# Two of eight router heads moved beside the next tile's attention, the other six on a new clock

## The reference, cut to what matters

```
def peer_ffn(h, wq, subkeys, u_tab, v_tab):      # 8 heads, 2 x 128 sub-keys, top 16 of each
    q = (hf @ wq).reshape(T, PEER_HEADS, 2, PEER_DKEY // 2)
    scores = jnp.einsum('thjd,hjkd->thjk', q, subkeys)
    top_s, top_i = lax.top_k(scores, PEER_TOPK)
    cand = top_s[:, :, 0, :, None] + top_s[:, :, 1, None, :]
    best_s, best_c = lax.top_k(cand.reshape(T, PEER_HEADS, PEER_TOPK * PEER_TOPK), PEER_TOPK)
    i1 = jnp.take_along_axis(top_i[:, :, 0], best_c // PEER_TOPK, axis=-1)
    i2 = jnp.take_along_axis(top_i[:, :, 1], best_c % PEER_TOPK, axis=-1)
    experts = i1 * PEER_KEYS + i2                 # 8 x 16 = 128 experts for each token
    gates = jax.nn.softmax(best_s, axis=-1)
    act = jax.nn.gelu(jnp.einsum('td,tkd->tk', xt, u_tab[et]))
    out = jnp.einsum('tk,tkd->td', gt * act, v_tab[et])
```

## Time and profile before

| what | value |
|---|---|
| median of three runs | 3264.56 us (3263.48 to 3269.51) |
| the profiled execution, its own time | 3259.96 us |
| its span | 3258.1 us |
| busy share of the span: PE, DVE, ACT, POOL | 72%, 72%, 46%, 36% |
| bytes by DMA, mean rate | 1317.83 MB, 404 GB/s |
| of them gathers of experts | 1073.81 MB, 1024 gathers |
| mean of one dot product on DVE (line 1870) | 1223 ns, 1024 of them |

### The profile page before, as it was taken

The page is one execution under the profiler, slowest core; times in us unless marked ns, Lnnn a source line. Parts: engine busy times, 40 slices in busy tenths (PEclk is TensorE's granted clock), DMA queues, the critical chain, the costliest instruction groups (busy, mean ns, idle before and its releaser), DMA issues.

```text
span 3258.1 us, 44723 instructions
## 1 busy us (share of the span) xinstructions
PE 2334.8 (72%) x15076; PEld 1157.1 (36%) x15076; DVE 2342.5 (72%) x6339; ACT 1496.1 (46%) x4877; POOL 1157.9 (36%) x1029
## 2 busy tenths in 40 slices
PE   7677777677775777767686678768778578866555
PEld 5363334243341434423243333424335143431111
DVE  6588856887668876688567975688766886588554
ACT  2215453355534455344543545344553446444443
POOL 0003343333433333333432434333443333334443
PEclk9788888888996988879888888878888798887777
DMA  9869999999999999999999999999999999999998
GB/s 371 362 249 380 412 421 419 404 411 420 420 418 410 404 419 383 419 402 418 421 419 416 404 420 421 419 405 406 420 413 419 403 417 421 418 414 397 422 421 341
DMA packets 206795, 1317.83 MB, mean 404 GB/s; under 512 B 26381, under 2 KB 42941, under 8 KB 53478
## 3 DMA queue, kind: packets, MB, share of 16 engines
q0 software_dynamic: 147456, 1073.81, 80.0%
q1 hardware_dynamic: 58390, 240.51, 18.5%
q10 hardware_dynamic: 720, 0.66, 0.1%
HBM read 1310.02 MB, written 7.16 MB: 404 GB/s over the span
## 4 chain that ended last, share of the span: by engine, by line
DMA 37%; PE 23%; DVE 22%; ACT 7%; issue 4%; POOL 3%; ACTq 0%; SPq 0%; POOLq 0%; DVEq 0%
DMA ringbuf<-in_p_uv,IDX 33%; PE PS L1010 12%; DVE ringbuf L1870 10%; POOL ringbuf L649 3%; PE PS L942 3%; DMA WB<-in_p_wi 3%; PE PS L786 2%; PE PS L972 2%; ACT v_th L1343 2%; ACT DIAG L1368 1%; ACT v_w L1361 1%; DVE I L1763 1%; PE PS L745 1%; DVE T L1761 1%; DVE ZB L1562 1%
## 5 line engine op out<-in xcount | busy, mean ns | idle before, releaser
L649 POOL DMA_INDIRECT ringbuf<-in_p_uv,IDX x1024 | 1157.6, 1130 | 2074.9 <-PE PS L1010 1684.2
L1010 PE MATMUL PS<-ringbuf,DIAG 64*64 64x512 f32 x8192 | 1292.3, 758 | 764.3 <-ACT DIAG L1368 734.3
L1870 DVE SCALAR_TENSOR_TENSOR ringbuf<-ringbuf,H 128x1024 f32<-128x1024 f32 x1024 | 1237.6, 1223 | 620.1 <-DMA ringbuf<-in_p_uv,IDX 611.3
L1010 PEld LDWEIGHTS PS<-ringbuf,DIAG 64*64 64x64 f32 x8192 | 310.7, 157 | 1468.5 <-ACT DIAG L1368 994.7
L1340 ACT ACTIVATE v_sq<-v_y 128x2 f32<-128x2 f32 x512 | 104.3, 204 | 1365.0 <-DVE ringbuf L1870 1334.9
L1343 ACT ACTIVATE v_th<-v_sq,v_y 128x1 f32<-128x1 f32 x1024 | 340.6, 380 | 17.2
L1361 ACT ACTIVATE v_w<-v_th,v_g 128x1 f32<-128x1 f32 x800 | 266.1, 379 | 38.4 <-ACT v_th L1343 1.1
L972 PEld LDWEIGHTS PS<-HT,WB 128*128 128x128 f32 x1856 | 222.3, 200 | 64.4 <-issue 56.6
L1368 ACT ACTIVATE DIAG<-fold,v_w 128x64 f32<-128x64 f32 x800 | 234.7, 340 | 13.0
L972 PE MATMUL PS<-HT,WB 128*128 128x128 f32 x1856 | 233.1, 286 | 2.0 <-DMA WB<-in_p_wq 2.0
L786 PE MATMUL PS<-WB,HT 128*128 128x256 f32 (+2 forms) x816 | 177.8, 373 | 48.6 <-DMA WB<-in_p_wi 48.6
(11 more groups left out here) (290 smaller groups left out, 2453.7 us busy)
## 6 DMA issues: line engine op xcount, KB each, us to landing
WB<-in_p_wq SPq DMA_DIRECT2D x58, 1024.0 KB
WB<-in_p_wi SPq DMA_DIRECT2D x37, 1024.0 KB
ringbuf<-in_p_ahead SPq DMA_DIRECT2D x20, 1024.0 KB, 10.9
WB<-in_p_ada SPq DMA_DIRECT2D x16, 1024.0 KB
WB<-in_p_wo SPq DMA_DIRECT2D x16, 1024.0 KB
ringbuf<-in_p_uv,IDX POOLq DMA_INDIRECT x1024
WF<-in_p_ada SPq DMA_DIRECT2D x12, 1024.0 KB, 13.8
WB<-in_p_wi SPq DMA_DIRECT2D x14, 768.0 KB
```

The costliest lines, as they stand in the source:

```text
L649: pool.indirect_dma_start(out=ring[n % RING], out_offset=None, in_=table, in_offset=bass.IndirectOffsetOnAxis(ap=IDX[:, k % 2, s:s + 1], a ...
L1010: mm = pe.matmul(PS[half:half + HALF, 2 * c + r, :], DIAG[r * HALF:(r + 1) * HALF, (n + q) % DIAGS, :], row[r * HALF:(r + 1) * HALF, D + c ...
L1870: dve.scalar_tensor_tensor(row, row, GELU_T, H2[:, k % 2, :], ALU.mult, ALU.mult, accum_out=Y[:, b, q:q + 1]).then_inc(dotted, 1)
```

## The change

1. The last lot (heads 6 and 7) of every tile but the last leaves `route` and becomes a generator `late` that DVE's attention loop of the next tile advances at nine of its steps (`LATE_AT`), each time behind that step's logits reduction. Its exponential on ACT moves to attention step i = 9 (`LATE_GATE`).
2. ACT writes the scores of heads 6 and 7 into the key buffers `SKT` instead of `SC`; SP waits with the first two key loads of the next tile until that lot is done. The late lot has buffers of its own (`T1L` and so on), 24,576 bytes into the work area, where `UT` and `PRJ` lie, which are free during the attention.
3. The remaining pieces get a clock of two rates: 3.2 units a pair up to step 56.5, 1.9 from there on. For tile 7, which keeps its four lots in `route`, this stretches the router further into phase 7.

```diff
-ROUTE_RATE = 3.14
+LATE = PH - BATCH
+ROUTE_AT, ROUTE_TURN, ROUTE_RATES = 44.5, 56.5, (3.2, 1.9)
+HEAD_COSTS, LOT_COSTS = (1.7, 1.7, 3.3), (1.0, 2.2, 3.4)
+LATE_AT = (0, 1, 2, 4, 5, 6, 8, 10, 12)
+LATE_GATE = 9
+def early_lots(j):
+    return lots_of(j)[:-1] if j + 1 < TILES else lots_of(j)
 def route_clock(j):
-    heads, lots, now = [], [], 0.0
...
+    clock, now = [], 0.0
+    dense = (ROUTE_TURN - ROUTE_AT) * ROUTE_RATES[0]
+    for h0, h1 in early_lots(j):
+        clock.append([])
+        for cost in HEAD_COSTS * (h1 - h0) + LOT_COSTS:
+            step = ROUTE_AT + now / ROUTE_RATES[0] if now <= dense else ROUTE_TURN + (now - dense) / ROUTE_RATES[1]
+            clock[-1].append(at(j, step + 1 if at(j, step) > PHASE[j] + 1 else step))
+            now += cost
+    return clock
...
             def keys(j, i):
+                if j and i < 2:
+                    sp.wait_ge(idx_done, lots_before(j))
...
                         if j:
-                            act.wait_ge(idx_done, lots_before(j))
+                            act.wait_ge(idx_done, lots_before(j) - 1)
...
+                    if j and i == LATE_GATE:
+                        gates(j - 1, len(lots_of(j - 1)) - 1)
...
                 def score_ev(i):
                     act.wait_ge(s_mm, PH * j + i + 1)
-                    act.activation(SC[:, 2 * i:2 * i + 2, :].rearrange("p h n -> p (h n)"), PS[:, 6 + i % 2, 0:WIDE],
-                                   ACT.Copy).then_inc(s_ev, 1)
+                    dst = SC[:, 2 * i:2 * i + 2, :].rearrange("p h n -> p (h n)") if i < LATE else SKT[:, i % 2, :]
+                    act.activation(dst, PS[:, 6 + i % 2, 0:WIDE], ACT.Copy).then_inc(s_ev, 1)
...
-                for i in range(2 * HEADS):
+                late = lot(j - 1, len(lots_of(j - 1)) - 1) if j else iter(())
+                next(late, None)
+                for i in range(2 * HEADS + 1):
                     yield at(j, 19 + i)
+                    if i == 2 * HEADS:
+                        next(late, None)
+                        break
...
                     if i == 7:
                         finish(0)
+                    if i in LATE_AT:
+                        next(late, None)
...
+            def lot(j, g):
+                if h0 >= LATE and j + 1 < TILES:
+                    t1, i1, i1f, b1, bc2, eq, ca, b2, b2f, ex = T1L, I1L, I1fL, B1L, BCL, EQL, CAL, B2L, B2fL, EXL
...
+                for h in range(h0, h1):
+                    for side in range(2):
+                        yield
+                        scores = SC[:, 2 * h + side, :] if h < LATE else SKT[:, h % 2, side * KEYS:(side + 1) * KEYS]
+                        top16(scores, t1[:, 2 * o + side, :], i1[:, 2 * o + side, :])
+                    yield
...
```

More of the change, by code:

```diff
@@ L188, in at, with gate_clock @@
     return START[j] + step
+def early_lots(j):
+    return lots_of(j)[:-1] if j + 1 < TILES else lots_of(j)
 def route_clock(j):
-    heads, lots, now = [], [], 0.0
-    def piece(cost):
-        nonlocal now
-        at_, now = at(j, 44.5 + now / ROUTE_RATE), now + cost
-        return at_ + 1 if at_ > PHASE[j] + 1 else at_
-    for h in range(PH):
-        heads.append([piece(cost) for cost in (1.7, 1.7, 3.3)])
-        if h + 1 in [e for _, e in lots_of(j)]:
-            lots.append([piece(cost) for cost in (1.0, 2.2, 3.4)])
-    return heads, lots
+    clock, now = [], 0.0
[7 more added lines that the diff above has]
+    return clock
+def gate_clock(j):
+    return [lot[-len(LOT_COSTS)] for lot in route_clock(j)]
 def ada_rows(j):
@@ L1142, in tile @@
                 owed = j > 0
-                last = route_clock(j - 1)[1][-1][0] if j else None
+                last = gate_clock(j - 1)[-1] if j else None
                 for step in range(2 if j == 0 else 0, 4):
@@ L1154, in tile @@
                     yield last
[L1155 removed]
+                    gates(j - 1, len(early_lots(j - 1)) - 1)
                 if j == 0:
@@ L1737, in tile, with step, top16 @@
                 yield from route(j)
-            def route(j):
-                nonlocal routed
-                l = j // T
-                heads, lots = route_clock(j)
-                now = heads[0][0]
-                def step(ins):
-                    nonlocal routed
-                    routed += 1
-                    ins.then_inc(route_step, 1)
+            def step(ins):
+                nonlocal routed
+                routed += 1
+                ins.then_inc(route_step, 1)
+            def top16(values, tops, places):
+                for half in range(2):
+                    part = slice(8 * half, 8 * half + 8)
+                    step(dve.max(tops[:, part], values))
+                    dve.wait_ge(route_step, routed)
+                    step(dve.max_index(places[:, part], tops[:, part], values))
+                    if half == 0:
+                        dve.wait_ge(route_step, routed)
+                        step(dve.match_replace(values, tops[:, part], values, LOWEST))
+                        dve.wait_ge(route_step, routed)
@@ L1750, in route, with next_norm @@
+            def route(j):
                 early = j + 1 < TILES
-                def next_norm():
+                def next_norm(now):
                     nonlocal early
@@ L1756, in next_norm @@
                         norm1(j + 1)
-                def top16(values, tops, places):
-                    for half in range(2):
-                        part = slice(8 * half, 8 * half + 8)
-                        step(dve.max(tops[:, part], values))
-                        dve.wait_ge(route_step, routed)
-                        step(dve.max_index(places[:, part], tops[:, part], values))
-                        if half == 0:
-                            dve.wait_ge(route_step, routed)
-                            step(dve.match_replace(values, tops[:, part], values, LOWEST))
-                            dve.wait_ge(route_step, routed)
@@ L1825, in route @@
-                for h in range(PH):
-                    now = heads[h][0]
-                    yield now
-                    next_norm()
-                    dve.wait_ge(s_ev, PH * j + h + 1)
-                    for side in range(2):
-                        top16(SC[:, 2 * h + side, :], T1[:, 2 * h + side, :], I1[:, 2 * h + side, :])
-                        now = heads[h][1 + side]
-                        yield now
-                        next_norm()
-                    dve.wait_ge(route_step, routed)
-                    for r0, r1, width, lo in ((0, STEEP, TOPK, 0), (STEEP, TOPK, STEEP, STEEP * TOPK)):
-                        step(dve.tensor_tensor(
-                            CA[:, lo:lo + (r1 - r0) * width].rearrange("p (a b) -> p a b", b=width),
-                            T1[:, 2 * h, r0:r1].unsqueeze(2).to_broadcast([P, r1 - r0, width]),
-                            T1[:, 2 * h + 1, 0:width].unsqueeze(1).to_broadcast([P, r1 - r0, width]), ALU.add))
-                    dve.wait_ge(route_step, routed)
-                    top16(CA[:, :], B1[:, h, :], BC[:, h, :])
-                    for g, (_, h1) in enumerate(lots_of(j)):
-                        if h1 == h + 1:
-                            now = lots[g][0]
-                            yield now
-                            next_norm()
-                            yield from batch(g)
@@ L1849, in route @@
+                for g, clock in enumerate(route_clock(j)):
+                    work = lot(j, g)
+                    next(work)
+                    for now in clock:
+                        yield now
+                        next_norm(now)
+                        next(work, None)
                 if early:
```

141 lines of the change are left out of this document (82 added, 59 removed).

## The result

| what | before | after |
|---|---|---|
| median, 20 runs each | 3264.40 us (3255.45 to 3272.06) | 3271.12 us (3263.68 to 3278.76) |
| profiled execution, its own time | 3259.96 us | 3267.65 us |
| its span | 3258.1 us | 3265.8 us |

What follows compares the result with a forecast made beforehand. DVE was taken to bound pairs 0 to 12, letting the DMA engines fall below 421 GB/s. The terms -24.5 - 2 + 10 + 3 = -13.5 us, from a median of 3264.6, gave 3251 us; range 3235 to 3272.

Steps and rivals of the forecast that it cites:

- The ceiling and the way of counting: Whole program: at most 421 GB/s, 1317.83 MB fixed; a stretch loses its length times (1 - rate / 421).
- The move and its size: Seven lots leave pairs 6 to 12: 18.1 us of DVE a phase, coming back whole in pairs 25 to 37.
- DVE is the bound there: Pairs 0 to 12: DVE finishes dot products late, slots come free late and the ring of eight runs dry.
- the 24.5 us: Pairs 0 to 12 of phases 1 to 7: gain taken as 0.8 of the 30.6 us lost there.
- what would stay: Behind pair 8: next tile's norm, a lot's first piece, a look-up; so 0.8 of 30.6 us was taken as gain.
- Phase 0, 2 us back: Phase 0, pairs 0 to 12: 2 us of its 8.1 us loss come back, between 0 and 5.
- Phase 2, 10 us: Phase 2, attention steps from step 4 on: late pieces on a saturated DVE cost 10 us, bounds 0 and 18.1.
- The other six phases, 3 us: Pairs 25 to 37 outside phase 2: late pieces cost 0.5 us a phase, 3 us; bounds 0 and 36.
- Rival 3: Attention steps become the bound: 4.5 us in each of six phases, 12.5 in phase 2; 3277 us; chance 0.18.
- rival 2: Pairs 0 to 12 slow for the handover, not the router: half comes back, -13, costs 13; 3264 us; chance 0.20.
- The Trainium skill's rule: HBM to SBUF: about 358 GB/s a core binds; that would give 3278 us; the prediction held the trace refutes it.

Runs made afterwards that it cites:

- Ten pads: After plus ten idle DVE reductions a phase behind pairs 6, 7, 9, 11 and 12 of phases 0 to 6: 1.0027 of before.
- taking the lot home: After with tile 2's last lot kept in its router on the old clock of 3.14 units a pair: 0.9993 of before, 3263.93 us.
- the combination: After with tile 2's last lot back in its router, the next tile's norm on DVE behind pair 7, router pieces at equal steps: 0.9984 of before, 3257.76 us.
- the norm experiments: Next tile's norm on DVE behind pair 7 instead of pair 8: in after 0.9998 of before, in before itself 1.0009.
- the norm edit: Next tile's norm on DVE moved from behind pair 8 to behind pair 7; alone in after, 0.9998 of before.

## Why the prediction was wrong

- **The ceiling and the way of counting: right.** 421 to 423 GB/s was the most in every window, and bytes were fixed. The losses differ by 6.4 us and the start-up by 1.3, the 7.7 us between the two profiled executions.
- **The move and its size: right.** DVE's busy time fell by 16 us in pairs 0 to 12 (phase 1, 68.28 to 52.24), for the 18.1 us of the lot.
- **"DVE is the bound there" and the 24.5 us that followed from it: wrong, and this is the step that failed.** The term measured as nothing (30.6 us before and after). I had read a busy share of 0.94 next to a low rate as cause and effect, over a window of thirteen pairs. The same rows held a sign against it: in phase 3 DVE is busy only 69.07 of 81.40 us, and the loss is 3.7 us, much as in the others. One window further down, before's loss sits in pairs 1 to 3 and 10. At 10 it comes from ACT waiting for the norm; both kernels have that wait (30.5 and 33.9 us). At the start of a phase the new clock put a lump of look-ups behind pair 62 and thinned the pieces behind pairs 0 and 3, so that pair 0 loses 5.1 us more and pairs 1 to 3 5.4 less. Ten pads that restore the load of pairs 6 to 12 cost 2.6 us, give or take 5, and not 20. The prediction named what would stay ("the next tile's norm, a lot's first piece and a look-up") and priced it at a fifth. In pairs 5 to 12 the norm alone was nearly all; in pairs 0 to 4 the copies gave 3.4 of 17.8 us when they were cut, and the close nothing when it was moved.
- **Phase 0, 2 us back:** it was 3.9, inside its bounds.
- **Phase 2, 10 us: right**, 8.6 us in its window, and taking the lot home gave 8.5 back, give or take 5.
- **The other six phases, 3 us: too high.** The three windows shown lose 0.2 to 0.3 us each, where before they lose 0 to 0.2, and pairs 25 to 44 of phases 1 and 3 to 6 lose 1.9 us in all for 1.7. Rival 3 with its 36 us did not happen.
- **The rivals.** It went as in rival 2 (the start is slow for the handover, not for the router), to which I gave 0.20, but its price was half the gain back, and the real one was none of it; so it ended above no change. That 3271 us still lies inside the stated range of 3235 to 3272 is luck: its upper end was there for rival 3, whose mechanism did not occur. The handover as a whole was not confirmed either, only the norm in it. What spoke for rival 2, phase 7's 398 GB/s without a next tile, was a sign for half of it: cut at pairs, that phase loses in pairs 0 to 3 and not at pair 10, where the others wait for the norm.
- **The Trainium skill's rule**, page "DMA: Bandwidth & Descriptors", section "Where 436 GB/s comes from", with its 358 GB/s on the HBM side: every window shown here lies above it, the starved ones too (371 and 374), and none is above 423. The section derives that figure as a stack's 716 GB/s divided by two cores, and this kernel runs on one; it also gives 425 GB/s for a transfer of 16 MB and calls it near the rate of the fabric, which the 421 to 423 here agree with.

What stays open: what makes the loss in pairs 0 to 4 beyond the lump (8.0 us of it are left in the combination, and lighter copies and a later close did not find it); why a saved wait is paid back later (pair 22 and pairs 33 to 38 in the norm experiments); and what the combination's 0.0016 is made of. Its edits alone gave 0.9993, 0.9998 and 1.0004 against 1.0019, which would add to -0.0062, and together gave -0.0035. A copy of the combination without the norm edit isn't told from it.

## What to carry to other kernels

A busy engine beside a starved resource is no proof. Cut the window to the smallest period of the kernel (here a pair) and see where in it the resource loses; then follow the release of one starved slot back. In this kernel, load that was taken away helped little unless it stood ahead of the instruction for which another engine waits. Idle instructions of known length, put at two different sets of places, told load from place in two runs; put everywhere at once, they could not.
